# Half-line offset of the low weight parts in a float32r two-block transformer kernel

## What is computed

```python
# first block
z = rmsnorm(x) @ w_in                     # phase in1, 2048 x 5200
x = x + concat(pool(z), attention(z)) @ w_out     # phase out1
up = rmsnorm(x) @ w_up                    # phase up1, 2048 x 11264
x = x + (silu(conv(up)[gate]) * conv(up)[val]) @ w_down   # phase down1
# second block
mod = silu(c) @ w_mod_2                   # 2048 x 12288, one row
... in2, out2, up2, down2 of the same kind, with gated linear attention
```

## Time and profile before

| | |
|---|---|
| median of 3 runs | 2222.65 us (2222.44 to 2222.78) |
| the profiled execution | 2222.8 us, of which 2220.7 us is the span of its instructions |
| TensorE (PE) busy | 2209.6 us, 11912 matmuls |
| weight loads (PEld) | 1914.3 us, beside the matmuls |
| VectorE | 1624.8 us |
| ScalarE | 1153.8 us |
| GpSimd | 69.2 us |
| DMA | 517.24 MB, 233 GB/s over the span |
| chain that ended last | 96% TensorE, 3% VectorE |

### The profile page before, as it was taken

The page is one execution under the profiler, slowest core; times in us unless marked ns, Lnnn a source line. Parts: engine busy times, 40 slices in busy tenths (PEclk is TensorE's granted clock), DMA queues, the critical chain, the costliest instruction groups (busy, mean ns, idle before and its releaser), DMA issues.

```text
span 2220.7 us, 31565 instructions
## 1 busy us (share of the span) xinstructions
PE 2209.6 (100%) x11912; PEld 1914.3 (86%) x11912; DVE 1624.8 (73%) x1916; ACT 1153.8 (52%) x1464; POOL 69.2 (3%) x47
## 2 busy tenths in 40 slices
PE   9999999999999999999999999999999999999998
PEld 9888888888888888888898888888888888888887
DVE  7779677788888877767766767787887666675555
ACT  6554546655555554444646545565555455554444
POOL 0004200000000000000000200000000000000000
PEclk9999999999999999999999999999999999999999
DMA  8767477578788876878575556757887655555553
GB/s 321 257 217 246 134 281 247 180 270 291 274 292 277 291 239 229 310 264 304 191 263 181 179 171 185 270 209 244 282 285 251 219 196 182 195 176 204 193 197 120
DMA packets 208104, 517.24 MB, mean 233 GB/s; under 512 B 12288, under 2 KB 46592, under 8 KB 183824
## 3 DMA queue, kind: packets, MB, share of 16 engines
q1 hardware_dynamic: 203456, 513.77, 66.9%
q10 hardware_dynamic: 4560, 2.25, 0.3%
HBM read 513.88 MB, written 2.11 MB: 232 GB/s over the span
## 4 chain that ended last, share of the span: by engine, by line
PE 96%; DVE 3%; ACT 0%; DMA 0%; issue 0%; SPq 0%; DVEq 0%; ACTq 0%
PE ps L2131 29%; PE ps L2140 15%; PE ps L2041 14%; PE ps L2043 14%; PE ps L2042 14%; PE ps L2161 4%; PE ps L2170 2%; DVE w_lo L1187 1%; DVE raw L1207 0%; PE ps L2575 0%; PE ps L2357 0%; PE ps L2351 0%; DMA raw<-in_w_in 0%; PE ps L2354 0%; PE ps L2431 0%; PE ps L2491 0%
## 5 line engine op out<-in xcount | busy, mean ns | idle before, releaser
L1187 DVE TENSOR_TENSOR w_lo<-raw,w_hi 128x1024 fp32r<-128x1024 f32 x758 | 939.2, 1249 | 534.2 <-ACT w_hi L572 533.5
L572 ACT ACTIVATE w_hi<-raw 128x1024 fp32r<-128x1024 f32 x758 | 790.8, 1057 | 908.1 <-PE ps L2043 352.2
L2131 PE MATMUL ps<-a_hl,w_hi 128*128 128x512 f32 x2684 | 625.7, 390 | 0.0
L2131 PEld LDWEIGHTS ps<-a_hl,w_hi 128*128 128x128 f32 x2684 | 498.1, 188 | 99.8
L2041 PE MATMUL ps<-w_hi,a_hl 128*128 128x512 f32 x1216 | 475.4, 391 | 0.0
L2043 PE MATMUL ps<-w_hi,a_hl 128*128 128x512 f32 x1216 | 473.3, 389 | 0.0
L2042 PE MATMUL ps<-w_lo,a_hl 128*128 128x512 f32 x1216 | 473.2, 389 | 0.0
L2140 PEld LDWEIGHTS ps<-a_hl,w_lo 128*128 128x128 f32 x2688 | 333.9, 192 | 6.7
L2140 PE MATMUL ps<-a_hl,w_lo 128*128 128x256 f32 x2688 | 336.2, 283 | 0.0
L2041 PEld LDWEIGHTS ps<-w_hi,a_hl 128*128 128x128 f32 x1216 | 228.3, 188 | 47.7 <-issue 0.7
L2043 PEld LDWEIGHTS ps<-w_hi,a_hl 128*128 128x128 f32 x1216 | 228.2, 188 | 47.7
(11 more groups left out here) (264 smaller groups left out, 1394.3 us busy)
## 6 DMA issues: line engine op xcount, KB each, us to landing
raw<-in_w_up SPq DMA_DIRECT2D x176, 1024.0 KB, 5.1
raw<-in_w_mod SPq DMA_DIRECT2D x96, 1024.0 KB, 5.3
raw<-in_w_down SPq DMA_DIRECT2D x88, 1024.0 KB, 5.0
raw<-in_w_in SPq DMA_DIRECT2D x86, 1024.0 KB, 5.3
raw<-in_w_out SPq DMA_DIRECT2D x32, 1024.0 KB, 6.2
x<-in_x SPq DMA_DIRECT2D x2, 1024.0 KB, 8.1
region<-gate_rows ACTq DMA_DIRECT2D x2, 1024.0 KB, 8.7
out_x<-x SPq DMA_DIRECT2D x8, 256.0 KB, 2.2
```

The lines of the kernel that those rows point to most:

```text
L572: nc.scalar.activation(hi_of(hh), raw[:, n % RAW_SLOTS, half * HALF:(half + 1) * HALF], ACT.Copy).then_inc(hi_ready, 1)
L1187: v.tensor_tensor(lo_of(hh), raw[:, n % RAW_SLOTS, half * HALF:(half + 1) * HALF], hi_of(hh).bitcast(F32), ALU.subtract).then_inc(lo_ready, 1)
L2131: mm = mmul(dst[:, BLOCK * ft:BLOCK * (ft + 1)], hi_of(hh, columns(kk, ft)), a[:, kts[kk], :, :].rearrange("p l s -> p (l s)"), start=firs ...
```

## The change

The buffer `w_lo` gets 16 floats (64 bytes) more per slot, and the halves of M and S pairs are written and read 8 floats (32 bytes) after the start of their slot. All other halves stay at the start of theirs. The start of slot `s` moves from `4096 s` to `4160 s` bytes behind the start of `w_lo`, and every buffer behind `w_lo` moves up by 256 bytes. No instruction is added, removed or put in another place.

```diff
+LINE = 16
...
-        w_lo = sb("w_lo", [P, HL_SLOTS, HALF], F32R)
+        w_lo = sb("w_lo", [P, HL_SLOTS, HALF + LINE], F32R)
...
             if hh in APART:
                 return region_r[:, APART[hh] + HALF + cols.start:APART[hh] + HALF + cols.stop]
-            return w_lo[:, hh % HL_SLOTS, cols]
+            off = LINE // 2 if hh in HALF_LINE_OFF else 0
+            return w_lo[:, hh % HL_SLOTS, cols.start + off:cols.stop + off]
...
+        HALF_LINE_OFF = {2 * PH[name].pairs[i].m0 + n for name in RUNS for a, b, layout in RUNS[name] if layout in ("M", "S")
+                         for i in range(a, b) for n in range(16)}
```

## The result

The changed kernel takes 2233.35 us (median of 6 runs, 2233.14 to 2233.65) against 2222.62 us for the kernel before (2222.44 to 2222.78). The ratio is 1.0047, with a 95% interval of 1.0037 to 1.0058: slower by 10.7 us, or 0.5%, with the interval clear of 1. The forecast was 2218.4 us with a range up to 2225.

A forecast was written before the change was run, and what follows sets the result against it. TensorE was taken as the bound, through its matmul steps. Terms of -4.9 (low matmuls), +0.16 (first pair of up1) and +0.56 (entering runs) summed to -4.2 us, giving 2218.4 us, range 2210 to 2225.

The forecast's parts named there:

- The bound: Whole kernel: TensorE is the bound and its feeders are early, so only the step of a matmul counts.
- The 3200 low matmuls: Lines 2140 and 2170, 256 columns, `w_lo` stationary, `a_hl` moving: 1.53 ns less per step, -4.9 us (bounds -35 to +18).
- the rows of `region`: Trace rows with one operand 32 bytes off: 256-column steps 1.2 to 1.7 ns shorter, 512-column steps 5.6 longer.
- The first pair of up1: 128 low matmuls with moving operand in `region`: both operands 32 bytes off, 4 runs from 3.79 to 3.83 us, +0.16 us.
- the sign that the prediction is wrong in its root: Line 2140 moves but the first pair of up1 does not: each operand's place counts, not the distance between them.
- Entering a run: Last 512-column matmul before each of 100 low runs meets an off-line load: 5.6 ns each, +0.56 us; at best 0.
- The writer: VectorE writes 416 halves 32 bytes off a line: nothing either way, and covered; 4 us at most without cover.
- the move by 256 bytes: All later buffers keep their place in a 64-byte line, `region` included: taken as 0.
- The pitch of the slots: Slots 1 and 3 of `w_lo`, moving in half of line 2042's 1216 T matmuls: taken as 0, ends +3.4 us and same below.
- the slower rival: Off-line loads in the 3200 low matmuls add 5.6 ns per step: +18 us, 2240.7 us; chance 0.12.
- the pitch rival: Longer slot pitch costs T matmuls +3.4 us, about what the offset gives: sum -0.8, 2221.9 us; chance 0.05.
- both rules of the Trainium skill: Weights have their own read port; memory lines are 16 bytes. By either, sum 0 and 2222.65 us; the nothing-happens rival, 0.13.

The follow-up runs named there:

- the offset alone: Against the kernel before: 392 of 416 M and S halves stored 32 bytes off at the old slot pitch, 256 empty bytes behind `w_lo`; 2220.53 us, ratio 0.9991.
- the pitch alone: Against the kernel before: slots of `w_lo` 64 bytes longer, no half moved off its slot's start, later buffers 256 bytes on; 2235.57 us, ratio 1.0058.
- the 64-byte offset: Against the kernel before: 392 M and S halves stored 64 bytes off at the old slot pitch, 256 empty bytes behind `w_lo`; 2216.56 us, ratio 0.9970.

## Why the prediction was wrong

- *The bound*: right. TensorE's waits did not change, and all of the difference is in its steps.
- *The 3200 low matmuls*: -4.9 was forecast, -4.4 measured (all 3328). The loads went to 188 ns and the duration to 280. The kernel that makes only this step, the offset alone, gives -4.7 for its 392 halves, so carrying the rows of `region` from a moving to a stationary operand worked there. In the changed kernel the match is in part luck. The halves lie 32, 96, 160 and 224 bytes off, not all 32, and -4.4 is a mean: in up1 a run takes 3.81 us and line 2131 beside it 7.31, in up2 3.77 and 7.27, where 3.78 to 3.80 was named for both. The pitch without any 32-byte offset shortens the low steps by 3.9 us as well.
- *The first pair of up1*: +0.16 forecast, 0 measured; its run stays at 3.79 us. Both operands lie 32 bytes off a 64-byte line there, and by the argument "both off is in step" the run should have gone back to 3.83. This was named ahead as the sign that the prediction is wrong in its root, since "then the place of each operand counts and not the distance between them". The runs show that a distance within a 64-byte line is not the rule: 64 bytes cost T 5 ns a step. Whether place or distance counts, taken over more bytes, no run separates.
- *Entering a run*: +0.56 forecast, +0.7 measured in the changed kernel, but as +1.1 in up1 and -0.4 in up2. With the offset alone it is +2.2 in M, since the exit from a run got dearer too, a cost that the prediction left out.
- *The writer* and *the move by 256 bytes*: nothing, as forecast; the move is measured by itself.
- *The pitch of the slots*: this is the step that failed. It took 0, with +3.4 us as the far end, and gave the case a chance of 0.05. Measured: +14.9 us in the changed kernel, and +12.9 net of a small gain in M for the pitch alone. The term was sized as 608 matmuls at 5.6 ns. The price of one was not too small, but the number of matmuls was, by a factor of six. Three slots of four are displaced, not two, since 128 bytes count in T (234 ns in the down phases). And the price falls on all three lines and on slot 0 too, 3648 matmuls at about 4 ns, since a displaced `w_lo` stream puts the streams beside it out of their rhythm. The trace held a hint: a 512-column run takes 7.28 us and not 32 x 226.7 ns = 7.25, and the 26 ns lie in the first five steps after each low run, although no operand of theirs is displaced. That is a neighbour's cost.
- *The rivals*: the slower rival placed its 18 us in the low matmuls, which got faster. The time came out slower by the mechanism of the pitch rival at over four times its price. By both rules of the Trainium skill that the prediction weighs ("TensorE: Matmul & The Clock Gate", section "Step-by-step: what each phase is for", and "SBUF — State Buffer", section "Specifications (TRN2)"), as it reads them, place would be without effect. The runs speak against that, by up to 14.5 us for nothing but `w_lo` 128 bytes further on.

## What to carry to other kernels

Where TensorE is the bound and loads a weight tile for each matmul, as here, the place of a buffer in SBUF is a parameter to try like a tile size. No rule came out that gives the best place; it was found by trying seven. Here 96 bytes for one layout gave 0.4%, and 64 bytes in the wrong place cost 0.5%. When a buffer is padded, list every reader and every slot of it: the part of a layout change that "does nothing" (here the pitch) slowed 3648 matmuls, the intended one sped up at most 3328. If a trace has the same operation at two places in memory, compare the steps, but take the price for all neighbours in the stream and not for the one operand.

## What the runs showed of the hardware

- Before the change, a step is 13 to 14 ns over the bare stream (106.7 ns for 256 columns, 213.3 for 512, worked out at 2.4 GHz) for 256 and for 512 columns. With `a_hl` moved by 64 bytes the excess ran from about 7 ns (113.4, the shorter low runs) to 20 ns (233.3, T steps).
- In the profiled run of the 64-byte offset TensorE waited 1.94 us near the start for VectorE, and the granted clock then fell to its lower level, 1.2 GHz, for 3.4 us. In the kernel before, where the longest wait of TensorE for VectorE there is 0.8 us, it stayed up. A window of that stretch with a clock of 0.50, and W matmuls of 256 columns in it:

```profile
12.00:14.00 2.00, 2.00 (x11) 2.00 (x10) 1.45 (x2) 2.00 (x5) 0.00 (x0) 0.50 1.04 402
...
12.51 0.41 PE L2072 MATMUL ps<-region_r,w_hi 128*128 128x256 f32 x1
12.72 0.41 PE L2073 MATMUL ps<-region_r,w_hi 128*128 128x256 f32 x1
12.94 0.41 PE L2074 MATMUL ps<-region_r,w_lo 128*128 128x256 f32 x1
```

 A step is 213 to 214 ns there, which is 256 columns at 1.2 GHz with no excess; W matmuls with the same operands are 118.3 ns at 2.4 GHz, 12 ns over the stream. So in these rows the excess is there at the upper level of the clock alone. The W sum of this execution is 104.4 us for it, in place of 102.2.
